# Expert results added by the scatter itself to a copy of the residual rows in memory

## The reference, cut to what matters

```
def _hmoe(x, ...):                       # n = 544 rows of 1024
    xn = _rmsnorm(x, g)
    ...                                  # group, two experts of it, weights: combine (n, 32)
    for e in range(N_EXPERTS):           # 32
        h = jax.nn.silu(xn @ w_gate[e]) * (xn @ w_up[e])         # 1024 -> 512, twice
        y = y + combine[:, e:e + 1] * (h @ w_down[e])            # 512 -> 1024
    return x + y
...
return _rmsnorm(x, g_final), ...
```

## Time and profile before

| | |
|---|---|
| time, median of 3 runs | 918.31 us |
| the profiled execution, its own time | 917.77 us |
| its span, first to last instruction | 916.2 us |
| PE busy | 803.4 us (88%) |
| DVE busy | 263.7 us (29%) |
| DMA, 16 engines, slices 19 to 37 of 40 | 424 to 429 GB/s, busy throughout |
| PE's share of the chain that ended last | 61% |
| DMA's share of that chain | 34% |

### The profile page before, as it was taken

The page is one execution under the profiler, slowest core; times in us unless marked ns, Lnnn a source line. Parts: engine busy times, 40 slices in busy tenths (PEclk is TensorE's granted clock), DMA queues, the critical chain, the costliest instruction groups (busy, mean ns, idle before and its releaser), DMA issues.

```text
span 916.2 us, 9588 instructions
## 1 busy us (share of the span) xinstructions
PE 803.4 (88%) x3838; PEld 456.1 (50%) x3839; DVE 263.7 (29%) x745; ACT 120.0 (13%) x230; POOL 128.0 (14%) x224
## 2 busy tenths in 40 slices
PE   2999999999999899959997797779778887888786
PEld 2788888778888655533333233233223332333332
DVE  3799756410011245451110111011101110111115
ACT  3210030120000223400000000000000000000012
POOL 3000005860033200010110101010101000100000
PEclk9999999999999999959998898899989898989898
DMA  9420121335200393149999999999999999999926
GB/s 313 128 93 24 69 104 37 109 129 180 92 1 0 140 425 130 47 157 428 424 429 426 428 426 426 426 427 426 427 427 426 426 426 429 426 427 428 378 69 253
DMA packets 41663, 251.58 MB, mean 275 GB/s; under 512 B 13061, under 2 KB 13913, under 8 KB 28786
## 3 DMA queue, kind: packets, MB, share of 16 engines
q1 hardware_dynamic: 34284, 236.97, 63.0%
q0 software_dynamic: 6672, 12.86, 3.9%
q10 hardware_dynamic: 662, 1.13, 0.4%
HBM read 245.33 MB, written 13.46 MB: 282 GB/s over the span
## 4 chain that ended last, share of the span: by engine, by line
PE 61%; DMA 34%; DVE 2%; issue 1%; ACTq 0%; ACT 0%; SPq 0%; DVEq 0%; POOLq 0%
DMA arena<-in_w_exp_up 32%; PE ps L1369 26%; PE ps L1619 12%; PE ps L1515 6%; PE ps L1632 5%; PE ps L1691 2%; PE ps L1454 1%; PE ps L1449 1%; PE ps L1611 1%; PE ps L1503 1%; PE ps L1537 1%; DVE arena L829 1%; DMA arena<-in_cache_pool 1%; ACTq L588 0%; DVE arena L782 0%
## 5 line engine op out<-in xcount | busy, mean ns | idle before, releaser
L1619 PE MATMUL ps<-arena 128*64 128x512 f32 x1024 | 256.7, 659 | 70.0 <-DMA arena<-in_w_exp_up 68.9
L1369 PE MATMUL ps<-arena 128*128 128x272 f32 x1024 | 238.8, 395 | 0.0
L1369 PEld LDWEIGHTS ps<-arena 128*128 128x128 f32 x1024 | 195.5, 191 | 39.8
L1619 PEld LDWEIGHTS ps<-arena 128*64 128x64 f32 x1024 | 86.9, 152 | 217.2 <-issue 215.1
L1632 PE MATMUL ps<-arena 128*64 128x512 f32 x512 | 116.4, 595 | 1.3 <-DVE arena L1280 1.3
L1284 DVE TENSOR_SCALAR arena<-ps,arena 128x512 f32<-128x512 f32 x32 | 24.0, 751 | 214.1 <-PE ps L1632 214.1
L782 DVE TENSOR_TENSOR arena<-arena 128x256 f32<-128x256 f32 (+10 forms) x223 | 75.5, 339 | 11.4 <-ACT arena L689 3.9
L1252 DVE TENSOR_TENSOR arena<-ps,arena 128x1024 f32<-128x1024 f32 x16 | 19.6, 1224 | 190.1 <-PE ps L1611 190.1
L1632 PEld LDWEIGHTS ps<-arena 128*64 128x64 f32 x512 | 37.9, 137 | 64.8 <-issue 61.4
L546 POOL DMA_INDIRECT y_parts<-arena x32 | 31.9, 997 | 267.8 <-DVE arena L1284 267.8
L732 ACT ACTIVATE arena<-ps,arena 128x512 f32<-128x512 f32 x32 | 22.0, 687 | 324.5 <-PE ps L1619 324.5
(11 more groups left out here) (222 smaller groups left out, 484.4 us busy)
## 6 DMA issues: line engine op xcount, KB each, us to landing
arena<-in_w_exp_gate SPq DMA_DIRECT2D x32, 2048.0 KB, 27.9
arena<-in_w_exp_up SPq DMA_DIRECT2D x32, 2048.0 KB, 32.3
arena<-in_w_exp_down SPq DMA_DIRECT2D x32, 2048.0 KB, 37.4
arena<-in_w_in SPq DMA_DIRECT2D x6, 2048.0 KB, 8.9
arena<-in_x_prompt SPq DMA_DIRECT2D x8, 512.0 KB, 6.6
arena<-in_w_out SPq DMA_DIRECT2D x2, 2048.0 KB, 10.2
arena<-y_parts SPq DMA_DIRECT2D x4, 1024.0 KB, 8.3
arena<-in_w_glu_a SPq DMA_DIRECT2D x1, 2048.0 KB, 10.5
```

Of the source, the lines that this page charges most:

```text
L1369: last = pe.matmul(dst[:, hh, 0:HALF], w[:, k, m * P:(m + 1) * P], rhs[:, k, hh * HALF:(hh + 1) * HALF], start=(k == 0), stop=(k == kk - 1))
L1619: last = pe.matmul(ps[n * TILE:(n + 1) * TILE, 2 + par, :], x_t[:, k, :], w[:, k, :], start=(k == 0), stop=(k == KD - 1))
```

## The change

Each token now has one row in DRAM, `y_sum` (two rows of 512 values), that starts as a copy of its residual row; every scatter adds to it. For that:

- POOL stores each tile of `x_tok` twice, to `x2_rows` and to `y_sum` (`sum_begin`). The second store of the last tile (tile 3, 512 KB) is issued after the first two gathers, and POOL waits for it before the experts' loop; DVE waits for it once, in expert 0, before it turns rows over that tile.
- A scatter reads its row of `y_sum`, adds and writes. Two scatters may meet in one row, so each waits until the one before has landed: `y_stored[(e - 1) % 2]` ahead of `y_ready`.
- The row numbers of `y_row` count two rows for each token, and the shift to a token number is by 1.
- Both read-backs of `x2_rows` (L411, L414), DVE's two additions for tile 4 and PE's 24 matmuls go. SP reads 4 KB a token in the place of 8 KB, and ACT and DVE take these rows from on-chip memory in the place of PSUM.

```diff
-        y_parts = nc.dram_tensor("y_parts", (4 * NT, F), F32).ap()
+        y_sum = nc.dram_tensor("y_sum", (2 * NT, F), F32).ap()
...
-            sp.wait_ge(x2_stored, 16 * TT)
-            sp.wait_ge(down_done, NE - 3)
-            sp.dma_start(ring[6].rearrange("p (i d) -> p i d", i=4),
-                         x2_rows[0:SEQ].rearrange("(i p) d -> p i d", p=P)).then_inc(x2_back, 16)
-            sp.wait_ge(gu_done, NE - 2)
-            sp.dma_start(x2_end[4][0:DEC], x2_rows[SEQ:NT]).then_inc(x2_back, 16)
+            sp.wait_ge(down_done, NE)
...
-                src = y_parts[4 * i * P:4 * (i * P + ROWS[i])].rearrange("(t k) n -> t (k n)", k=4)
+                src = y_sum[2 * i * P:2 * (i * P + ROWS[i])].rearrange("(t h) n -> t (h n)", h=2)
                 sp.dma_start(y_end[i][:ROWS[i]], src).then_inc(y_back[i], 16)
...
+            def sum_begin(i):
+                dst = y_sum[2 * i * P:2 * (i * P + ROWS[i])].rearrange("(t h) n -> t (h n)", h=2)
+                pool.dma_start(dst, x_tok[:ROWS[i], i, :]).then_inc(sum_begun, 16)
+
             for n, i in enumerate(OUT_ORDER):
                 pool.wait_ge(x2_ready, 2 * n + 2)
                 pool.dma_start(x2_rows[i * P:i * P + ROWS[i]], x_tok[:ROWS[i], i, :]).then_inc(x2_stored, 16)
+                if n + 1 < TT:
+                    sum_begin(i)
...
             pool.wait_ge(x2_stored, 16 * TT)
+            pool.wait_ge(sum_begun, 16 * (TT - 1))
             pool.wait_ge(rows_ready, 1)
             for j in range(3):
                 if j == 2:
+                    sum_begin(OUT_ORDER[-1])
                     pool.wait_ge(xt_done, 1)
                 gather(j)
+            pool.wait_ge(sum_begun, 16 * TT)
             for e in range(NE):
...
+                if e:
+                    pool.wait_ge(y_stored[(e - 1) % 2], 16 * ((e - 1) // 2 + 1))
                 pool.wait_ge(y_ready, e + 1)
                 pool.indirect_dma_start(
-                    out=y_parts, out_offset=bass.IndirectOffsetOnAxis(ap=y_row[:, e:e + 1], axis=0),
-                    in_=y_sb[e % 2], in_offset=None, bounds_check=4 * NT - 1, oob_is_err=False).then_inc(y_stored[e % 2], 16)
+                    out=y_sum, out_offset=bass.IndirectOffsetOnAxis(ap=y_row[:, e:e + 1], axis=0),
+                    in_=y_sb[e % 2], in_offset=None, bounds_check=2 * NT - 1, oob_is_err=False,
+                    compute_op=ALU.add).then_inc(y_stored[e % 2], 16)
...
                 if n:
-                    act.wait_ge(sum_done, n)
                     act.wait_ge(squares3, n)
-                    src = ps[:r, 2 * i:2 * i + 2, :]
-                else:
-                    act.wait_ge(sample_sum, 2)
-                    src = x2_end[i][:r].rearrange("p (h n) -> p h n", h=2)
...
+                act.wait_ge(y_back[i], 16)
+                act.activation(junk2[:r], y_end[i][:r], ACT.Square, accum_out=ss[:r, i:i + 1]).then_inc(squares3, 1)
...
+                    if j == 1:
+                        dve.wait_ge(sum_begun, 16 * TT)
...
-            for k in range(2):
-                x_i = x2_end[last][:ROWS[last]]
-                dve.tensor_tensor(x_i, x_i, y_end[last][:ROWS[last], k * D:(k + 1) * D], ALU.add).then_inc(sample_sum, 1)
-                dve.wait_ge(sample_sum, k + 1)
...
-            for i in END_ORDER[1:]:
-                pe.wait_ge(y_back[i], 16)
-                add(i, y_end[i][:, 0:D], False, False)
-                add(i, y_end[i][:, D:2 * D], False, True).then_inc(sum_done, 1)
```

More of the change, by code:

```diff
@@ L213, in encoder_step @@
         y_sb = [at(O_YSB + n * F, F) for n in range(2)]
-        x2_end = [ring[6][:, i * D:(i + 1) * D] for i in range(4)] + [ring[7][:, 0:D]]
-        y_end = [ring[8 + i // 2][:, i % 2 * 2 * D:(i % 2 + 1) * 2 * D] for i in range(4)] + [ring[7][:, D:3 * D]]
+        y_end = [ring[6][:, i * D:(i + 1) * D] for i in range(4)] + [ring[7][:, 0:D]]
         junk2 = ring[5][:, 0:D]
@@ L300, in encoder_step @@
         ov_done, ov_seen, y_all = sem("overflow_done"), sem("overflow_seen"), sem("y_all")
-        x2_back, y_back = sem("x2_back"), [sem(f"y_back{i}") for i in range(TT)]
-        sample_sum, sum_done, squares3, mean3, root3, final_ready = sem("sample_sum"), sem("sum_done"), sem("squares3"), sem("mean3"), sem("root3"), sem("final_ready")
+        sum_begun, y_back = sem("sum_begun"), [sem(f"y_back{i}") for i in range(TT)]
+        squares3, mean3, root3, final_ready = sem("squares3"), sem("mean3"), sem("root3"), sem("final_ready")
         def psum_waits(eng, name):
@@ L432, in _ @@
                 dst = out["y_prompt"][0, i * P:(i + 1) * P] if i < 4 else out["y_sample"][0]
-                sp.dma_start(dst, x2_end[i][:ROWS[i]]).then_inc(outs_done, 16)
+                sp.dma_start(dst, y_end[i][:ROWS[i]]).then_inc(outs_done, 16)
             sp.wait_ge(hist_out, 32)
@@ L517, in _ @@
                       allow_small_or_imprecise_dtypes=True)
-            pool.iota(row_no, pattern=[[4 * P, TT], [2, 2]], base=1, channel_multiplier=4,
+            pool.iota(row_no, pattern=[[2 * P, TT], [0, 2]], base=1, channel_multiplier=2,
                       allow_small_or_imprecise_dtypes=True)
@@ L574, in more @@
                 pool.indirect_dma_start(
-                    out=y_parts, out_offset=bass.IndirectOffsetOnAxis(ap=ov_y_row, axis=0),
-                    in_=y_sb[0], in_offset=None, bounds_check=4 * NT - 1, oob_is_err=False).then_inc(ov_y, 16)
+                    out=y_sum, out_offset=bass.IndirectOffsetOnAxis(ap=ov_y_row, axis=0),
+                    in_=y_sb[0], in_offset=None, bounds_check=2 * NT - 1, oob_is_err=False,
+                    compute_op=ALU.add).then_inc(ov_y, 16)
                 pool.wait_ge(ov_y, n * 16)
@@ L758, in _ @@
                 if n:
-                    act.wait_ge(sum_done, n)
                     act.wait_ge(squares3, n)
-                    src = ps[:r, 2 * i:2 * i + 2, :]
-                else:
-                    act.wait_ge(sample_sum, 2)
-                    src = x2_end[i][:r].rearrange("p (h n) -> p h n", h=2)
-                act.activation(junk2[:r].rearrange("p (h n) -> p h n", h=2), src,
-                               ACT.Square, accum_out=ss[:r, i:i + 1]).then_inc(squares3, 1)
+                act.wait_ge(y_back[i], 16)
+                act.activation(junk2[:r], y_end[i][:r], ACT.Square, accum_out=ss[:r, i:i + 1]).then_inc(squares3, 1)
                 act.wait_ge(mean3, n + 1)
@@ L1241, in _ @@
                 part = slice(64 * half, 64 * half + 64)
-                last = dve.tensor_scalar(x_row[part], by_pair[part, :, half], 2, None, ALU.logical_shift_right)
+                last = dve.tensor_scalar(x_row[part], by_pair[part, :, half], 1, None, ALU.logical_shift_right)
             last.then_inc(rows_ready, 1)
@@ L1305, in more @@
                 dve.wait_ge(ov_y_idx, n)
-                dve.tensor_scalar(ov_x_row, ov_y_row, 2, None, ALU.logical_shift_right).then_inc(ov_idx, 1)
+                dve.tensor_scalar(ov_x_row, ov_y_row, 1, None, ALU.logical_shift_right).then_inc(ov_idx, 1)
                 x_out(0, n + NP, TILE)
@@ L1313, in _ @@
             dve.wait_ge(g_in, 32)
-            dve.wait_ge(x2_back, 32)
-            last = END_ORDER[0]
-            dve.wait_ge(y_back[last], 16)
-            for k in range(2):
-                x_i = x2_end[last][:ROWS[last]]
-                dve.tensor_tensor(x_i, x_i, y_end[last][:ROWS[last], k * D:(k + 1) * D], ALU.add).then_inc(sample_sum, 1)
-                dve.wait_ge(sample_sum, k + 1)
             for n, i in enumerate(END_ORDER):
@@ L1328, in _ @@
                 inverse_root(mean, root_i)
-                x_i, g_i = (x.rearrange("p (h n) -> p h n", h=2) for x in (x2_end[i][:r], g_b[:r]))
-                dve.scalar_tensor_tensor(out=x_i, in0=ps[:r, 2 * i:2 * i + 2, :] if n else x_i, scalar=root_i,
-                                         in1=g_i, op0=ALU.mult, op1=ALU.mult).then_inc(final_ready, 1)
+                dve.scalar_tensor_tensor(out=y_end[i][:r], in0=y_end[i][:r], scalar=root_i, in1=g_b[:r],
+                                         op0=ALU.mult, op1=ALU.mult).then_inc(final_ready, 1)
         @block.tensor
```

## The result

The changed kernel takes 928.63 us in the median of 4 runs (927.52 to 930.35), the kernel before 918.46 us in the same session. The ratio is 1.0101, 95% interval 1.0084 to 1.0118: slower by 1.0%. The forecast was 925.5 us, range 916 to 935, slower with 0.76. The profiled execution took 927.52 us, its span is 925.8 us against 916.2 before.

A forecast was written before the change was run, and what follows sets the result against it. The prediction took the DMA engines to bound the stretch from 410 us to the last weights, and PE the last stage. The second read's +11.3 us and the last stage's -4.1 us gave +7.2 us: 925.5 us, range 916 to 935.

The forecast's parts named there:

- Part 1, the second read: Full DMA stretch: scatters reading their rows add 11.3 us, between 9.8 on the mean engine and 12.7 on the slowest.
- the share of the slowest engine: Full DMA stretch: the engine serving most rows carries 1.3 times the mean, making the second read 12.7 us.
- the shortfall of the last windows: End of the weight stream: DMA share below full in three windows, 6.2 us, read as the slowest engine's lag.
- small packets cost more than bytes: Full DMA stretch: the second read costs 15 to 20 us, time 929 to 935 us; chance 0.13.
- The second read is free: Full DMA stretch: the second read costs 0 to 2 us, time 913 to 916 us; chance 0.13.
- a case of 0: Full DMA stretch, lower bound: 0 us if a row's second read runs beside the write made anyway.
- Part 2, the five stores: Out projection and first gathers: the stores to `y_sum` cost 0 us, at most 1.2 us.
- Part 3, the serial wait: Experts' loop: each scatter waiting for the one before costs 0 us; POOL's idle time still ends by DVE.
- Part 4, the read-backs: Behind the last weights on SP's queue: dropping 2.2 MB of residual reads gains 0 us, since nothing waits for them.
- Part 5, the last stage: After the last scatter: without PE's additions DVE sets the pace, 2.8 us a tile; gain 4.1 us, 1.5 to 5.1.

The follow-up runs named there:

- experiment 5: The kernel before with every scatter done twice, the second time to a tensor nobody reads: 933.15 us, ratio 1.0148.
- run 3: The kernel before with an expert's slots in another order, its tokens spread evenly over groups of four partitions: 916.64 us, ratio 0.9966.
- experiments 3 and 4: Slots spread evenly over groups of four partitions, in the kernel before (916.64 us, ratio 0.9966) and in the changed kernel (918.83 us, ratio 0.9985).
- experiments 4 and 6: With spread slots: the changed kernel (918.83 us, ratio 0.9985), and the kernel before with every scatter done twice (927.34 us, ratio 1.0091).
- experiment 1: The changed kernel with plain scatters in place of adding ones, all waits and stores kept: 914.59 us, ratio to the kernel before 0.9948.
- experiment 2: The kernel before with each scatter also waiting for the landing of the one before: 919.3 us, ratio 0.9995.

## Why the prediction was right, and by how much it was off

**The bounds were read rightly.** The stretch is set by the DMA engines and each byte has its price: experiment 5 added 4.46 MB of plain writes and the time rose by 1.5%. The last stage was set by PE, and without PE by DVE.

**Part 1, the second read: mechanism right, size too small.** Forecast 11.3 us, from 9.8 on the mean engine and 12.7 on the slowest. Measured 14.5, or 13.7 against the kernel without the addition. The term that was sized wrong is the share of the slowest engine, 1.3 times the mean. I took the shortfall of the last windows, 6.2 us, as its lag. That sum is only the mean shortfall up to 875 us, with the read-back of the residual, 5.2 us of work for each engine, still inside it. The ends show more: the last `down` load landed at 870.8 us (39.3 us after its issue at 831.5), and from 860 us on the windows hold 8.8 us of work, 3.6 without the read-back, a mean end near 863.6 and a lag of 7.2 us (863.4 and 7.4 in the expectation of run 3). And half of the way from the mean to the slowest was no value to take, since by the prediction's own sentence a load has landed only when its part on the slowest engine has. The runs give 14.5/9.8 = 1.48, or 13.7/9.8 = 1.40 for the addition alone, with the rows piled up, and 10.4/9.8 = 1.06 with them spread. That the factor is the load of one engine is argued, as said at experiments 3 and 4.

The rival "small packets cost more than bytes" falls by experiments 4 and 6: with the rows spread both kinds cost 10.3 to 10.4 us where bytes alone give 9.8. "The second read is free" falls by experiment 1. The rule of the Trainium skill (Collectives: The Full Stack, "The bandwidth ceiling"), two source reads on one ring and no price for the arithmetic, was weighed with a case of 0 beside it; runs 1, 5 and 6 bear out the price for a scatter, 13.7 us for either kind of row; the ring they can't show.

**Part 2, the five stores: 0, as forecast** (15.35 us an interval with them, 15.32 without; the 0.8 us at most of experiment 1 are as large with the wait alone, in experiment 2).

**Part 3, the serial wait: at most 0.9 us in the stretch, but not as told.** I wrote that POOL's idle time would still end by DVE, and that it would be wrong if a scatter ended it. A scatter ended it 10 times in 32. The time didn't suffer beyond that, since DVE needs a buffer only two experts later: all of DVE's idle time ahead of L1286 ended by PE. The test was too strict. At the very end it does cost 0.3 us: the last two scatters are 5.54 us apart, one takes 4.79 us to land, and the last is issued 1.12 us after its data is ready, 0.34 us later than before. I had taken 0 there, with the landing of a plain scatter.

**Part 4, the read-backs: no gain, as forecast.** In the kernel without the addition they are gone, and the last `up` load lands 0.8 us later than before, not sooner.

**Part 5, the last stage: forecast 4.1 us, measured 5.5.** From the last scatter to SP's reads 4.5 us (forecast 4.6). The first read took 2.36 us in place of 3.3, half the bytes, which I had left at the old value. The chain of tile 4 took 3.9 us, as forecast. Then products 2.65 us apart, not 2.8: I had added a gap to 2.74 where DVE's next mean starts before the product has ended. The rows of tiles 0 and 1:

```profile
913.49 1.28 DVE L1326 SCALAR_TENSOR_TENSOR arena<-arena 128x1024 f32<-128x1024 f32 x1
914.69 0.15 DVE L1322 TENSOR_SCALAR arena<-arena 128x1 f32<-128x1 f32 x1
916.14 1.28 DVE L1326 SCALAR_TENSOR_TENSOR arena<-arena 128x1024 f32<-128x1024 f32 x1
```

The two errors of size, 3.2 us and 1.4 us, had opposite signs, so that the sum came out nearer than its first term by luck: +14.5 - 5.5 is 9.0 where 7.2 was forecast, and the median of the runs is 3.1 us above the forecast's 925.5. Of the 9.6 us of span the other 0.6 aren't the change's.

## What to carry to other kernels

An accumulating DMA isn't free where the DMA engines are full: count it as two plain rows, and look at the share and the packets and not at the GB/s, since the second read isn't among the profile's bytes. It moves work from an idle stretch, where it was visible, into the full one, where nothing waits for it by name. And where rows are gathered and scattered by partition and only some partitions are in use, try to deal them out over groups of four; here that was worth 0.3% without another instruction that matters, measured twice, and about 1.1% in the changed kernel.

## What was not expected of the hardware

The clock granted to PE early in the out projection differs from run to run of programs that are the same up to there, and moves all that follows. From 310 to 320 us, the kernel before and the changed one (last three columns clock, DMA share, GB/s):

```profile
310.00:320.00 10.00, 8.29 (x81) 4.69 (x82) 3.06 (x15) 3.41 (x9) 2.85 (x10) 1.00 0.76 291
```
```profile
310.00:320.00 10.00, 8.16 (x78) 4.36 (x79) 2.72 (x12) 1.95 (x5) 3.36 (x11) 0.83 0.75 289
```

PE had stood idle for 2.87 us before this in both. The same 64 matmuls then took 3.66 us in one and 5.02 in the other, the lower of PE's two levels for part of them. Over all runs the first gather started between 398.6 and 402.1 us, which is more than some of the effects that were looked for; what sets it stays open. An indirect scatter with an addition holds POOL for 1.56 us, without one for 1.0.
